# Both high passes of a two-group chunk ahead of both low passes, in the products of the first block

## What is computed

```python
def mla_mixer(...):      return o.reshape(b, s_len, MLA_HEADS * MLA_V) @ w_o          # 1024 x 1024
def dilated_mixer(...):  qkv = (h @ w_qkv).reshape(b, s_len, DIL_GROUPS, 3, ...)       # 1024 x 9216
                         return o.reshape(b, s_len, ...) @ w_o                         # 1024 x 1024
def swiglu(h, w_in, w_out):
    gu = h @ w_in                                                                      # 1024 x 5632
    return (jax.nn.silu(gu[..., :D_FF]) * gu[..., D_FF:]) @ w_out
```

## Time and profile before

| what | value |
|---|---|
| time, median of 3 runs | 3225.29 us (3223.66 to 3227.65) |
| time of the profiled execution | 3223.79 us |
| its span, first to last instruction | 3222.1 us |
| PE busy | 2832.7 us, 88% |
| PEld (weight loads of PE, beside it) | 1889.3 us, 59% |
| DVE, ACT, POOL busy | 1282.1, 916.5, 1042.7 us |
| HBM traffic over the span | 238 GB/s |

### The profile page before, as it was taken

One profiled execution on the slowest core, in us unless ns is written; L12 is line 12 of the kernel. 1 busy time (PEld: TensorE's weight loads), 2 busy tenths in 40 slices (PEclk: granted clock), 3 DMA queues, 4 the chain that ended last, 5 costly groups with the idle time before them and its releaser, 6 DMA issues. The chain is left out here.

```text
span 3222.1 us, 33958 instructions
## 1 busy us (share of the span) xinstructions
PE 2832.7 (88%) x13329; PEld 1889.3 (59%) x13329; DVE 1282.1 (40%) x2416; ACT 916.5 (28%) x1276; POOL 1042.7 (32%) x431
## 2 busy tenths in 40 slices
PE   7899879999898898698997999998597897999885
PEld 4777757777677676477875444443475674433331
DVE  5622142444323423664245333333516545333223
ACT  0433322224333312432212222222314332222221
POOL 0277646642677344033430000000354572000000
PEclk9999989999899999899998999999698998999998
DMA  5545488872454453212332999999333357999996
GB/s 190 176 151 166 157 293 284 293 246 66 154 170 158 144 170 128 80 66 81 105 131 105 371 422 422 422 422 416 110 105 102 120 186 282 412 422 422 422 422 268
DMA packets 208912, 746.02 MB, mean 232 GB/s; under 512 B 13876, under 2 KB 15074, under 8 KB 158832
## 3 DMA queue, kind: packets, MB, share of 16 engines
q1 hardware_dynamic: 189872, 669.61, 54.9%
q0 software_dynamic: 18880, 74.22, 6.8%
HBM read 721.00 MB, written 44.27 MB: 238 GB/s over the span
## 5 line engine op out<-in xcount | busy, mean ns | idle before, releaser
L1754 POOL TENSOR_TENSOR weight_ring_r<-weight_ring,weights_high_r 128x2048 fp32r<-128x2048 f32 x136 | 621.4, 4579 | 509.4 <-ACT weights_high_r L1389 419.3
L1389 ACT ACTIVATE weights_high_r<-weight_ring 128x2048 fp32r<-128x2048 f32 x136 | 257.6, 1902 | 730.5 <-PE banks L755 325.7
L750 PE MATMUL banks<-weights_high_r,x_transposed_r 128*128 128x512 f32 x1008 | 403.0, 400 | 37.2 <-ACT weights_high_r L1389 13.2
L1879 POOL DMA_DIRECT2D moe_y<-arena x64 | 34.2, 535 | 923.3 <-DVE arena L2580 923.3
L755 PE MATMUL banks<-weight_ring_r,x_transposed_r 128*128 128x512 f32 x1328 | 324.5, 390 | 3.1 <-POOL weight_ring_r L1754 3.1
L1754 POOL TENSOR_TENSOR weight_ring_r<-weight_ring,gates_r 128x2048 fp32r<-128x2048 f32 (+1 forms) x60 | 271.0, 4526 | 135.0 <-ACT gates_r L1389 73.9
L755 PEld LDWEIGHTS banks<-weight_ring_r,x_transposed_r 128*128 128x128 f32 x1328 | 249.3, 188 | 57.6 <-POOL weight_ring_r L1754 5.7
L750 PEld LDWEIGHTS banks<-weights_high_r,x_transposed_r 128*128 128x128 f32 x1008 | 193.5, 192 | 92.3 <-issue 26.4
L751 PE MATMUL banks<-weights_high_r,arena_r 128*128 128x512 f32 x520 | 205.0, 394 | 0.0
L1608 ACT ACTIVATE arena<-banks 64x1024 f32<-64x1024 f32 x64 | 65.3, 1020 | 488.1 <-PE banks L1148 488.1
L2565 DVE TENSOR_TENSOR arena<-banks,arena 64x1024 f32<-64x1024 f32 x64 | 78.2, 1222 | 294.2 <-ACT arena L1608 294.2
(11 more groups left out here) (387 smaller groups left out, 4727.2 us busy)
## 6 DMA issues: line engine op xcount, KB each, us to landing
weight_ring<-in_moe_w_up SPq DMA_DIRECT2D x64, 1024.0 KB, 18.2
x_transposed<-in_moe_w_up SPq DMA_DIRECT2D x60, 1024.0 KB, 18.4
tokens_out<-in_moe_w_down SPq DMA_DIRECT2D x60, 1024.0 KB, 16.3
arena<-in_moe_w_gate SPq DMA_DIRECT2D x60, 1024.0 KB, 17.9
weight_ring<-in_moe_w_down SPq DMA_DIRECT2D x60, 1024.0 KB, 16.6
weight_ring<-in_w_in SPq DMA_DIRECT2D x56, 1024.0 KB, 5.2
weights_high<-in_moe_w_gate SPq DMA_DIRECT2D x56, 1024.0 KB, 17.8
weight_ring<-in_w_ada SPq DMA_DIRECT2D x48, 1024.0 KB, 7.5
```

The lines of the kernel that those rows point to most:

```text
L750: nc.tensor.matmul(banks[t][:, 0:width], xh, wh[:, k, :], start=k0 + k == 0, stop=False)
L1389: nc.scalar.activation(high(s, kn, width), slot(c, kn, width), ACT.Copy).then_inc(high_ready, 1)
L1754: nc.gpsimd.tensor_tensor(slot(c, kn, width, ring_r), slot(c, kn, width), high(s, kn, width), ALU.subtract).then_inc(low_ready, 1)
L1879: nc.gpsimd.dma_start(ys_dram[e * CAP:(e + 1) * CAP, :], A[own(e), E_Y:E_Y + D]).then_inc(ys_out[e % 2], 16)
```

## The change

Chunks n > 0 of a split product of the first block with two groups go through the new `two_groups`: it takes the banks of both tiles, waits for the high part of the first group and issues its high pass, does the same for the second group, then waits for the low part of the first group and issues its low pass, which ends with `w_used`, then the second group's, which ends with `acc_ready` for each tile. Matmuls, their operands and the waits are the same in number. Products of the second block and products with another number of groups stay with `group`.

```diff
--- before.py
+++ after.py
@@ -759,6 +759,31 @@
                 if k0 + kn < g.k_tiles:
                     last.then_inc(w_used, 1)
 
+            def two_groups(g, n, lhs, width):
+
+                split = g.first_split[n]
+                banks = [acc_bank() for _ in range(g.tiles)]
+                for i, (k0, kn) in enumerate(g.groups):
+                    pe.wait_ge(high_ready, split + i + 1)
+                    wh = high(split + i, kn, width)
+                    for t in range(g.tiles):
+                        for k in range(kn):
+                            xh, xl = lhs(k0 + k, t)
+                            nc.tensor.matmul(banks[t][:, 0:width], xh, wh[:, k, :], start=k0 + k == 0, stop=False)
+                            nc.tensor.matmul(banks[t][:, 0:width], xl, wh[:, k, :], start=False, stop=False)
+                for i, (k0, kn) in enumerate(g.groups):
+                    pe.wait_ge(low_ready, split + i + 1)
+                    wl = slot(chunk[0], kn, width, ring_r)
+                    chunk[0] += 1
+                    for t in range(g.tiles):
+                        for k in range(kn):
+                            last = nc.tensor.matmul(banks[t][:, 0:width], lhs(k0 + k, t)[0], wl[:, k, :],
+                                                    start=False, stop=k0 + k == g.k_tiles - 1)
+                        if i == 1:
+                            last.then_inc(acc_ready, 1)
+                    if i == 0:
+                        last.then_inc(w_used, 1)
+
             def first_chunk(g, lhs, turned):
 
                 width = g.chunks[0][1]
@@ -819,6 +844,9 @@
                     return
                 col, width = g.chunks[n]
                 banks = []
+                if g in block_one and g.split and len(g.groups) == 2:
+                    two_groups(g, n, lhs, width)
+                    return
                 for i, (k0, kn) in enumerate(g.groups):
                     if g.split:
                         group(g, lhs, banks, chunk[0], g.first_split[n] + i, k0, kn, width)
```

## The result

The changed kernel is slower: 3275.98 us median (3270.18 to 3284.14, 4 runs) against 3226.47 us, a ratio of 1.0155 with a 95% interval of 1.0132 to 1.0179. That is 50 us; 42 were forecast. Its profiled execution took 3276.69 us, 52.9 more than that of before.

The account below looks back on a forecast made before the run. g_dil's reload loop, 12.79 us beside PE's 14.32, was to bind once the release came 3.62 us later. Loop 30.2, crowded DMA 1 and clock 11 made 42 us over the profiled 3223.79: 3266 us, range 3251 to 3285.

Parts of the forecast that it names:

- The bound: g_dil: PE looks full, 229.38 of 234.59 us, but beside its 14.32 us period runs a 12.79 us reload loop.
- (a): Wait for the first low part moves from 16 to 32 matmuls in; g_dil's POOL waits, 3.1 us, can end.
- (b): Wait for the second high part comes 1.85 us earlier; in g_ff_in that part is ready a chunk ahead.
- (c): First slot's release comes 3.62 us later; g_ff_in has at least 4 us free, cost 0; single chunks 0.
- (d): g_dil: loop becomes 16.41 us against PE's 14.32, PE waits 2.09 us ahead of each chunk, 30.2 us together.
- (e): Ahead of g_dil's chunk 1: later load joins full DMA engines, start 0 to 2.7 us later, 1 taken.
- (f): g_dil: low clock behind four long gaps and 2 or 3 of 12 short ones, 11 us.
- All other stages equal within 1 us: Sign expected outside g_dil: every other stage keeps its time to within 1 us.
- Rival 1: g_dil's loop binds, but the clock holds behind most gaps: 30 to 33 us, 3255 us, chance 0.20.
- Rival 2: g_dil's loop binds, nearly every gap brings low clock or second high part is late: 58 us, 3282, chance 0.10.
- Rivals 3 and 4: g_dil: reload stays off the path, 3219 us, chance 0.03; or the release does not matter, 3224, chance 0.03.
- the narrow reading: Clock in g_dil: gaps between dense matmuls cost nothing beside themselves, so the sum would be 31 us, not 42.

Follow-up runs that it names:

- the dose: Release delay varied in the new order: 1.8 us later gave +6.9 us, 3.6 (the change) +50, 5.2 gave +92, each against the kernel before.
- the release without the order: Kernel before with its old pass order, only the first slot's release told behind the second high pass: 3280.05 us against 3226.91, ratio 1.0174.
- all but g_dil: Kernel before with the new order in every changed chunk except g_dil's: 3228.42 us, ratio 1.0000.
- half dose: Changed kernel with the first low pass between the second high pass's two tiles, release 1.8 us later than before: 3233.82 us against 3226.91, ratio 1.0020.
- large dose: Changed kernel with the release behind the last but one low matmul, 5.2 us later than before: 3323.53 us against 3231.04 before, ratio 1.0286.
- filled kernel: Changed kernel plus 18 unneeded transposes ahead of each g_dil chunk's wait for the high part: 3266.42 us against 3280.72 for the changed kernel.
- the splitting: Two kernels against the one before, new order only in g_dil or everywhere else: ratios 1.0136 and 1.0000.
- the kernel before with the gaps filled: Kernel before plus unneeded transposes at PE's waits in first chunks and ahead of g_dil's chunk 1: 3220.41 us against 3227.13, ratio 0.9981.
- g_dil alone: Kernel before with the new order only in g_dil's 17 chunks: 3270.05 us against 3226.91, ratio 1.0136.

## Why the prediction was right, point by point

**The bound.** That PE's 98% in g_dil hid a loop with 1.5 us of slack was right, and is shown by the dose: +6.9 us for half the delay, +50 for the whole.

**(a) and (b), the waits.** The waits for POOL went. In g_dil this is worth more than the 3.1 us I read off, since the release without the order has a period 1.0 us longer. My 16.41 us had no such wait in it, so the sum holds.

**(c) Cover in g_ff_in and the single chunks.** Right: 0, by the kernel with all but g_dil (1.0000, interval of 0.15%, 5 us, to each side) and the 11.37 us between chunks. The 4 us of cover were not tested by themselves.

**(d) The loop.** Forecast 16.41 us, measured 16.5 to 16.6 in the undisturbed periods of chunks 8, 10, 13, 15 and 16. Three of its terms were too small. First, the load of the first slot: I took 5.02 us for all; thirteen of the 16 took 5.01 to 5.38, three 6.09, 6.11 and 6.39, and all together were 5 us longer than forecast. Second, the second group's load. I took 5.9 us, near the lower end of 5.0 to 7.5; it took 6.6 to 7.9, 6.9 in the middle. Its time goes with how close it follows the first one: issued 5.4 us behind it, as before the change, it took 5.0 to 5.3 us; 3.6 to 3.8 us behind it (half dose) 5.0 to 5.3 in 13 of 16; 1.8 to 2.0 us 6.6 to 7.9; and 0.4 us in 15 of the 16 of the large dose 7.3 to 8.0. It used up most of the slack that I had seen and made PE wait 0.4 us twice in the middle of a chunk. The right row was that of the ada pairs (median 7.5), which I had kept for the other end. Third, the step from ACT's end to PE's start: 0.05 us from one row of before, 0.14 in all 16 chunks after (as 587.79 + 1.91 to 589.84).

**(e) The crowd ahead of chunk 1.** I took 1 us, and none is seen: the wait ahead of chunk 1 is 9.86 us where it was 10.02, and the chunk starts at 447.45 in place of 447.85. In the other profiles it starts between 444.6 and 455.3, so 1 us can't be told from the spread.

**(f) The clock.** Forecast 11 us, from 4 to 10 slow stretches. In the first profile of the changed kernel there are three beside the one at chunk 1, and PE was at the low level for 18.6 us of chunk 1 to 17 (5.0 of them at the start of chunk 1, as before); in the second there are seven, and 38.7 us. Half of the added time is 7 and 17 us, but it costs only where it delays the release: without low clock the load is issued 9.4 us behind the chunk's start, and with it up to 2.8 us later. These delays add up to 5.7 us in the first profile (2.7, 1.6 and 1.4 in the chunks 3, 4 and 12) and 14.2 in the second. So the term was in the middle of what it does, but as one number it was false precision: it differs between executions by about as much as itself. The reasoning behind it failed. There were seven long gaps in each, not four, since the three late loads made short ones long; of these, 3.0 to 3.4 us, only two in the first profile and five in the second brought the low clock, so nine of nine in the trace of before (by a recount it has more, all with a slow stretch) didn't carry over, and why is open. Of the nine short ones, one of 2.23 us, ahead of 503.42, brought it in the first profile and two in the second. For these I had taken the gap of 2.08 us as the nearest row, which had no slow stretch behind it. The same trace has a nearer one with the other answer: an idle time of 1.92 us, with one of 1.71 us ahead of it, and the low clock behind it.

```profile
1064.58 0.28 PE L883 MATMUL banks<-constants,ada_columns 128*32 128x128 f32 x1 [1.71 <-DVE small L1921]
1066.78 3.51 PE L883 MATMUL banks<-constants,scaled_rows 128*128 128x128 f32 x16 [1.92 <-DVE scaled_rows L1982]
```

```profile
1067.10:1070.50 3.40, 3.19 (x16) 2.57 (x13) 2.04 (x4) 2.93 (x10) 0.00 (x0) 0.50 0.06 24
```

**Outside g_dil.** "All other stages equal within 1 us" failed: up to 9 us, most of it following the clock, in stages that the change doesn't touch. I had looked for what the change does to them and not for how much they vary by themselves. The executions of before lie between 3216 and 3238 us.

**The sum.** In the first profile g_dil's 43.7 us are the 30.2 of the loop, 5.7 of the clock ahead of the release (forecast 11), 5.5 of longer first loads up to ACT's start, 1.4 of late second parts in the chunks 5 and 6, 1.4 of the step from ACT to PE (all forecast 0), less 0.7 because the release comes 0.05 us earlier than forecast; 0.2 are left over. (e) is 0 (forecast 1), and 9 lie outside (forecast 0), to 53. The median of 50 is in the range. That is the right mechanism with two errors that partly cancel: in this profile the clock was taken 5 us too large, and the loads and steps 8 us too small. The mis-sized terms are the loads', 5.02 and 5.9 us against 5.3 and 7.0 on average, and the clock.

**Rivals.** Rival 1 (hardly any low clock) is what the filled kernel looks like: 3266.42 - 3231.04 = 35 us, near its 30 to 33. Rival 2 is what the larger dose looks like. Rivals 3 and 4 are ruled out by the dose and by the splitting.

**The rule on the clock.** In the changed kernel the low stretches at 640.2 and 483.2 began within idle times of 3.13 and 3.40 us that had dense matmuls ahead of them; gaps of 3.14 and 3.07 us, ahead of 607.41 and 692.55, brought none. So such a gap may cost more than itself or not. The Trainium skill (TensorE: Matmul & The Clock Gate, Part 1) names an idle window as what ends the full rate. By the narrow reading of that in the prediction the fill would have gained nothing in g_dil, and its stretch was 4 and 11 us shorter.

## What to carry to other kernels

A wait that is moved off one engine's path moves every signal behind it. Ask who is released by the work that you push back, and how long that one's way round is: release, load, preparation, first use. Compare it with the period in each stage by itself, since the same code had some 4 us to spare in one stage, by my estimate, and 1.5 in the other. When the release moves, also ask how close together the loads behind it are now issued. And price idle time of TensorE with what it does to the clock behind it, then compare with the kernel's own spread: work that nobody needs, put in the gap, was a gain here, of 4 to 11 us in one stage of the changed kernel and of some 7 us in the kernel before.

## What the hardware showed beside that

Idle times of PE as short as 2.13 us (ahead of 628.81 in the second profile of the changed kernel) and 1.84 us (ahead of 830.67 in the kernel before with the gaps filled) were followed by 3.4 us at 1.2 GHz, while some of 3.0 us and more in the first were not. Over the executions of the kernel before, this seems to make a large part of the spread of 22 us (argued from the mean clock of each of 23 executions, whose correlation with the time is -0.8, and not tested by itself; the two profiles of before show that there is another part).

Three of the 16 loads that g_dil waits for in the first profile of the changed kernel took 1 us longer than the rest. In each of them an instruction fetch shares the DMA engines, as the queues of the stretch 599.2 to 605.3 show:

```profile
q1 hardware_dynamic: 763, 1.53, 79.7%
q8 instruction: 1, 0.02, 1.5%
```

The same three loads are the late ones in the second profile of the changed kernel (6.46, 6.33 and 6.39 us) and with g_dil alone (6.38, 5.89 and 6.16), each with a fetch, and so were the two late second loads of the half dose. But other loads had a fetch beside them and were not late (5.17 us here), and the kernel before has one of 6.73 us without a fetch, so the link is not settled.

A DVE addition between two SBUF tiles ended only with a running POOL pass. Before the change, the one that finishes an ada piece took 4.20 us and ended at 570.93, POOL's pass at 570.90; in the changed kernel, where POOL is idle at that time, the same one takes 0.17 us:

```profile
566.73 4.20 DVE L2485 TENSOR_TENSOR ada_columns<-small,ada_bias 128x8 f32<-128x8 f32 x1
...
566.29 4.61 POOL L1754 TENSOR_TENSOR weight_ring_r<-weight_ring,weights_high_r 128x2048 fp32r<-128x2048 f32 x1 [4.64 <-ACT weights_high_r L1389]
```

```profile
587.07 0.17 DVE L2513 TENSOR_TENSOR ada_columns<-small,ada_bias 128x8 f32<-128x8 f32 x1
```

These rows stand for the others: of the 16 such additions between chunk 1 and 17 before the change, the 11 that began during a POOL pass took 3.71 to 4.54 us and ended within 0.03 us of its end, and the other five, like all 16 after the change, took 0.17 us. It costs nothing here, as DVE is not on the path. But it is why DVE's busy time in g_dil, 92.93 us before and 55.50 after, fell with nearly the same instructions: the 11 hold 43.4 us.
